# The last MoE column cut to two experts, its rows kept by quarters on partition groups and added to the tokens by 32-row products

## What is computed

```
x = rmsnorm(h_res)                                  # (512, 1024)
each token: the best of 4 groups, in it the best 2 of 8 experts, weights comb
for every expert e:  act = silu(x @ wg[e]) * (x @ wu[e]) * comb[:, e]
                     y  += act @ wd[e]              # wg, wu 1024x256, wd 256x1024
out = rmsnorm(h_res + y) * final_norm
```

## Time and profile before

| what | value |
|---|---|
| median of 3 runs | 498.78 us (497.97 to 499.63) |
| the profiled execution's own time | 497.26 us |
| its span | 495.4 us |
| mean granted clock of PE in the span | 0.989 of full speed |
| PE busy | 468.2 us (95%) |
| DVE busy | 282.6 us (57%) |
| ACT busy | 149.6 us (30%) |
| DMA bytes | 143.00 MB, mean 289 GB/s |

### The profile page before, as it was taken

The page is one execution under the profiler, slowest core; times in us unless marked ns, Lnnn a source line. Parts: engine busy times, 40 slices in busy tenths (PEclk is TensorE's granted clock), DMA queues, the critical chain, the costliest instruction groups (busy, mean ns, idle before and its releaser), DMA issues.

```text
span 495.4 us, 10550 instructions
## 1 busy us (share of the span) xinstructions
PE 468.2 (95%) x4290; PEld 312.1 (63%) x4290; DVE 282.6 (57%) x698; ACT 149.6 (30%) x367; POOL 37.3 (8%) x45
## 2 busy tenths in 40 slices
PE   7999999999999999998999999999999999885785
PEld 5888899888796544554656555655665555453442
DVE  4799999999967985248374422333342222132256
ACT  3450237630166333330244222221222121112134
POOL 0000000000001000000012021101202111000000
PEclk9999999999999999999999999999999999889999
DMA  8991000000008999539887999999999999999994
GB/s 270 351 370 61 1 0 2 1 1 1 3 3 278 413 427 426 251 103 415 324 305 266 420 384 429 422 420 424 419 425 420 424 419 425 422 425 425 419 372 182
DMA packets 29089, 143.00 MB, mean 289 GB/s; under 512 B 4357, under 2 KB 11685, under 8 KB 20336
## 3 DMA queue, kind: packets, MB, share of 16 engines
q1 hardware_dynamic: 23360, 131.03, 65.6%
q0 software_dynamic: 5248, 10.85, 6.2%
q10 hardware_dynamic: 432, 0.44, 0.3%
HBM read 133.21 MB, written 16.78 MB: 303 GB/s over the span
## 4 chain that ended last, share of the span: by engine, by line
PE 71%; DMA 17%; DVE 5%; SPq 4%; issue 1%; ACT 1%; DVEq 0%; ACTq 0%; POOLq 0%
PE bank_pair L1577 13%; PE bank_pair L1916 11%; PE bank_pair L1778 9%; DMA area_g<-in_w_exp 8%; DMA area_w<-in_w_exp 7%; PE bank_pair L1939 5%; PE bank_pair L1587 4%; PE bank_pair L1924 4%; PE bank_pair L1527 3%; SPq L519 3%; PE bank_pair L1715 3%; DVE area_m L934 2%; PE bank_pair L1909 2%; PE bank_pair L1947 2%; PE bank_pair L1542 1%; PE bank_pair L2369 1%
## 5 line engine op out<-in xcount | busy, mean ns | idle before, releaser
L1778 PE MATMUL bank_pair<-area_w,area_m 128*128 128x512 f32 x128 | 57.0, 595 | 0.0
L934 DVE SCALAR_TENSOR_TENSOR area_m<-area_g,cols,area_m 128x512 f32<-128x512 f32 x60 | 41.3, 744 | 0.0
L1778 PEld LDWEIGHTS bank_pair<-area_w,area_m 128*128 128x128 f32 x128 | 23.5, 190 | 26.0 <-issue 26.0
L1916 PE MATMUL bank_pair<-area_w,area_m 128*64 128x256 f32 x320 | 38.5, 383 | 1.4 <-DMA area_w<-in_w_exp 1.0
L1916 PE MATMUL bank_pair<-area_g,area_m 128*64 128x256 f32 x256 | 32.0, 393 | 2.1 <-DMA area_g<-in_w_exp 1.9
L1916 PEld LDWEIGHTS bank_pair<-area_w,area_m 128*64 128x64 f32 x320 | 22.4, 137 | 16.0 <-issue 5.9
L2152 DVE COPY cst<-bank_pair 128x128 f32<-128x128 f32 (+1 forms) x36 | 9.5, 263 | 36.0 <-PE bank_pair L1930 29.5
L2170 DVE COPY area_m<-bank_pair 64x512 f32<-64x512 f32 x20 | 13.9, 694 | 22.8 <-PE bank_pair L1939 22.8
L1916 PEld LDWEIGHTS bank_pair<-area_g,area_m 128*64 128x64 f32 x256 | 18.0, 139 | 13.9 <-issue 5.6
L2159 DVE TENSOR_TENSOR cst<-cst,bank_pair 128x128 f32<-128x128 f32 x22 | 6.4, 289 | 32.6 <-ACT cst L2073 32.6
L2161 DVE TENSOR_TENSOR cst<-cst,bank_pair 64x128 f32<-64x128 f32 x18 | 5.3, 293 | 32.0 <-ACT cst L2075 31.9
(11 more groups left out here) (443 smaller groups left out, 875.3 us busy)
## 6 DMA issues: line engine op xcount, KB each, us to landing
area_g<-in_w_exp SPq DMA_DIRECT2D x14, 2048.0 KB
area_w<-in_w_exp SPq DMA_DIRECT2D x13, 2048.0 KB, 37.8
area_w<-in_w_exp SPq DMA_DIRECT2D x16, 1024.0 KB, 8.3
area_g<-in_w_exp SPq DMA_DIRECT2D x14, 1024.0 KB
area_x<-in_w_exp SPq DMA_DIRECT2D x4, 2048.0 KB, 25.4
area_w<-in_w_in SPq DMA_DIRECT2D x6, 1024.0 KB, 14.1
area_w<-in_w_out SPq DMA_DIRECT2D x2, 2048.0 KB, 14.9
expert_out<-area_g SPq DMA_DIRECT2D x2, 2048.0 KB, 22.8
```

The costliest lines, as they stand in the source:

```text
L934: ins = V.scalar_tensor_tensor(out=mixT[:, i, :], in0=src, scalar=w, in1=mixT[:, i, :], op0=ALU.mult, op1=ALU.add)
L1778: ins = T.matmul(bank[7][:, :], mixT[:, k, j * P:(j + 1) * P], w_out_sb[:, n, k, :], start=(k == 0), stop=(k == KT - 1))
L1916: ins = T.matmul(out_b[h * BC:(h + 1) * BC, 0:2 * P], x[:, k, :], w_gate_up[slot][:, :, k, h * P:(h + 1) * P], start=(k == 0), stop=(k == ...
```

## The change

Columns 14 and 15 change places: the one with four light experts comes first (blocks 34 to 37) and is scattered, and the last has two (blocks 38 and 39; `OWN` is 38). A result of the last column keeps the form that `down_small` gives it: quarter q of the 1024 outputs on partitions 32q to 32q+31. So ACT copies it in one instruction (`y_quarters`), and `mix` is turned once for each of the two experts onto all four partition groups (`last_rows_turned(n)`, 16 small matmuls in blocks 35 and 37, and a copy by DVE each). The rows are added by 32-row products of 256 columns on the four row groups (`last_rows(n, j, q)`): 16 for each expert. Ten of the first expert's go between blocks 38 and 39 (`rows_before_last`), four behind block 39's gate and up, and two with the second expert's 16 behind its down product (`rows_of_last`). PSUM is laid out anew in two tensors of four banks; block 39 does all its work in bank 7. The residuals of tiles 0 and 2 go in before block 38's gate and up (three quarters) and behind its down product. The reads get semaphores by expert, tile 3's residual is read ahead of tile 2's rows, tile 2's first read is added by PE, the additions are whole tiles on DVE, and the tiles end in the order 1, 0, 2, 3. `keep_warm` goes. The core of the diff:

```diff
-    plan += [mid[1], light[0], heavy[0], heavy[1], light[1], heavy[2], mid[2], heavy[3], mid[3], mid[4], light[3], light[2]]
+    plan += [mid[1], light[0], heavy[0], heavy[1], light[1], heavy[2], mid[2], heavy[3], mid[3], mid[4], light[2], light[3]]
...
+        bank_quad = [ctx.enter_context(nc.psum_tensor(f"bank_quad{i}", [P, 2048], F32)) for i in range(2)]
+        bank = [bank_quad[i // 4][:, i % 4 * 512:(i % 4 + 1) * 512] for i in range(8)]
...
+        of_quarter = [gathered[:, n * SEQ:(n + 1) * SEQ] for n in range(2)]
...
-            def last_rows_turned():
-                dve.wait_ge(mix_turned, 1)
-                V.tensor_copy(mix_flat, bank[7][:, :]).then_inc(mix_ready, 1)
+            def last_rows_turned(n):
+                dve.wait_ge(mix_turned, 3 + n)
+                V.tensor_copy(of_quarter[n], bank[7][:, :]).then_inc(mix_ready, 1)
...
-        MIX_BANK = ((2, 3), (1, 6), (7, 0), (4, 5))
         AHEAD_TILE = 1
         BACK = (AHEAD_TILE, 0, 2, 3)
-        total = bank_pair[2][:, :]
-        weight_of = area_x[:, 0:2 * P].rearrange("p (k n) -> p k n", k=2)
+        FINAL = (AHEAD_TILE, 0, 2, 3)
+        QUARTER = D // 4
+        total = [bank_quad[0][:, :].rearrange("p (n c) -> p n c", n=4)[:, :, j * QUARTER:(j + 1) * QUARTER] for j in range(2)]
+        total += [bank_quad[1][:, j * D:(j + 1) * D].rearrange("p (n c) -> p n c", n=4) for j in range(2)]
+        yq = [area_m[:, 2 * KT * P + LAST % 2 * D + n * QUARTER:2 * KT * P + LAST % 2 * D + (n + 1) * QUARTER] for n in range(2)]
+        weight_of = area_x[:, 0:3 * P].rearrange("p (k n) -> p k n", k=3)
+        d_back = [[d_win[j] for j in range(NT)], d_x]
         ROOM_FROM = max(LAST_OF[RING - 1::RING]) + 1
-        SUMS = 2 * ET
...
+        def gu_bank(b_):
+            return bank[b_ % 2][:, 0:2 * P] if b_ < NB - 1 else bank[7][:, 0:P]
+        def turn_bank(b_):
+            return bank[4] if b_ < NB - 1 else bank[7][:, P:]
+        def down_bank(b_):
+            return bank[5 + b_ % 2] if b_ < NB - 1 else bank[7][:, QUARTER:]
...
-                if with_resid and j == ET:
-                    queue.dma_start(xr[j], resid[j * P:(j + 1) * P, :]).then_inc(d_spill, 16)
+                if with_resid and j == 2:
+                    queue.dma_start(xr[ET], resid[ET * P:, :]).then_inc(d_spill, 16)
                 for k in range(2):
-                    queue.dma_start(ye[k][:, j, :], expert_out[k * SEQ + j * P:k * SEQ + (j + 1) * P, :]).then_inc(d_x[j], 16)
+                    queue.dma_start(ye[k][:, j, :], expert_out[k * SEQ + j * P:k * SEQ + (j + 1) * P, :]).then_inc(d_back[k][j], 16)
...
-            for j in range(NT):
-                sp.wait_ge(o_ready, j + 1)
+            for i, j in enumerate(FINAL):
+                sp.wait_ge(o_ready, i + 1)
...
-            for b_ in range(OWN, NB):
-                y_out(b_ - 1)
-                silu_of(b_)
+            def y_quarters(b_):
+                act.wait_ge(dn_done, b_ + 1)
+                if b_ == OWN:
+                    act.wait_ge(d_sc[LAST % 2], sent(LAST - 2))
+                A_.activation(yq[b_ - OWN], down_bank(b_)[:, 0:QUARTER], ACT.Copy).then_inc(y_lo, 1)
+            y_out(OWN - 1)
+            silu_of(OWN)
+            y_quarters(OWN)
+            silu_of(NB - 1)
             act_turned(NB - 1)
-            y_both(NB - 1)
+            y_quarters(NB - 1)
...
-            for j in range(ET):
-                act.wait_ge(summed, j + 1)
-                row_stats(j, 0, xr[j])
-            act.wait_ge(mixed, 2 * ET + 1)
-            row_stats(ET, 0, total)
+            for i, j in enumerate(FINAL[:ET]):
+                act.wait_ge(summed, i + 1)
+                row_stats(i, j, by_quarter(xr[j]))
+            act.wait_ge(mixed, ALL_ROWS + 2)
+            row_stats(ET, ET, total[ET])
...
+                V.tensor_scalar(weight_of[:, 2, :], ident, w_rest[:, 0, 2:3], None, ALU.mult).then_inc(diag_ready, 1)
...
-                if b_ == MIX_AT + NT + 1:
-                    last_rows_turned()
+                if b_ == OWN - 2:
+                    last_rows_turned(0)
...
-            for b_ in range(OWN, NB):
-                act_turned(b_ - 1)
-                y_out(b_ - 1)
-                gated(b_)
-                if b_ == NB - 2:
-                    row_weights()
+            act_turned(OWN - 1)
+            y_out(OWN - 1)
+            gated(OWN)
+            row_weights()
+            last_rows_turned(1)
+            act_turned(OWN)
+            gated(NB - 1)
...
             def rows_ahead(j):
-                dve.wait_ge(d_x[j], 16 + 32)
                 for k in range(2):
+                    dve.wait_ge(d_back[k][j], 32)
                     V.scalar_tensor_tensor(out=xr[j], in0=ye[k][:, j, :], scalar=w_rest[:, k, j:j + 1], in1=xr[j],
                                            op0=ALU.mult, op1=ALU.add).then_inc(first_sum, 1)
                     dve.wait_ge(first_sum, k + 1)
             def last_added(j):
-                dve.wait_ge(mixed, 2 * j + 2)
...
+                dve.wait_ge(mixed, ALL_ROWS)
+                V.tensor_tensor(by_quarter(xr[j]), total[j], by_quarter(xr[j]), ALU.add).then_inc(summed, 1)
             def token_sums(j):
-                dve.wait_ge(d_x[j], 16 + 32)
...
+                dve.wait_ge(d_back[0][j], 32)
+                dve.wait_ge(mixed, ALL_ROWS)
+                V.scalar_tensor_tensor(out=by_quarter(xr[j]), in0=by_quarter(ye[0][:, j, :]), scalar=w_rest[:, 0, j:j + 1],
+                                       in1=total[j], op0=ALU.mult, op1=ALU.add).then_inc(first_sum, 1)
+                dve.wait_ge(d_back[1][j], 32)
+                dve.wait_ge(first_sum, SUMS)
                 V.scalar_tensor_tensor(out=xr[j], in0=ye[1][:, j, :], scalar=w_rest[:, 1, j:j + 1], in1=xr[j],
                                        op0=ALU.mult, op1=ALU.add).then_inc(summed, 1)
+            def second_added(j):
+                dve.wait_ge(d_back[1][j], 32)
+                dve.wait_ge(mixed, ALL_ROWS + 1)
+                V.scalar_tensor_tensor(out=by_quarter(xr[j]), in0=by_quarter(ye[1][:, j, :]), scalar=w_rest[:, 1, j:j + 1],
+                                       in1=total[j], op0=ALU.mult, op1=ALU.add).then_inc(summed, 1)
...
             rows_ahead(AHEAD_TILE)
+            last_added(AHEAD_TILE)
             token_sums(0)
-            last_added(AHEAD_TILE)
-            token_sums(2)
-            for j in range(ET):
-                row_norm(j, 0, xr[j])
-            row_norm(ET, 0, total)
+            row_norm(0, AHEAD_TILE, by_quarter(xr[AHEAD_TILE]))
+            second_added(2)
+            row_norm(1, 0, by_quarter(xr[0]))
+            row_norm(2, 2, by_quarter(xr[2]))
+            row_norm(ET, ET, total[ET])
...
-            def last_rows_turned():
+            def last_rows_turned(n):
                 pe.wait_ge(mix_made, NT)
+                pe.wait_ge(mix_ready, 2 + n)
                 for j in range(NT):
-                    ins = T.transpose(bank[7][:, j * P:(j + 1) * P], mix[:, j, :], ident)
+                    for q in range(4):
+                        ins = T.matmul(bank[7][q * 32:(q + 1) * 32, j * P:(j + 1) * P], mix[:, j, n * 32:(n + 1) * 32], ident,
+                                       start=True, stop=True, tile_position=(0, q * 32))
                 ins.then_inc(mix_turned, 1)
...
-            def keep_warm(n, width):
...
+            def resid_in(j, h, start):
+                T.matmul(bank_of(j, h), ident, xr[j][:, h * 512:(h + 1) * 512], start=start, stop=False)
+            def resid_quarter(q):
+                T.matmul(total[0][:, q, :], ident, by_quarter(xr[0])[:, q, :], start=True, stop=False)
+            def last_rows(n, j, q, start=False, stop=False):
+                p = slice(q * 32, (q + 1) * 32)
+                return T.matmul(total[j][:, q, :], of_quarter[n][p, j * P:(j + 1) * P], yq[n][p, :],
+                                start=start, stop=stop, tile_position=(q * 32, 0))
...
+            def rows_of_choice(k, j, weight, stop):
+                for h in range(2):
+                    ins = T.matmul(bank_of(j, h), weight, ye[k][:, j, h * 512:(h + 1) * 512], start=False, stop=stop)
+                return ins
+            def rows_before_last():
+                last_rows(0, 2, 0)
+                last_rows(0, 3, 1, start=True)
+                last_rows(0, 2, 2).then_inc(mixed, 1)
+                for q in range(4):
+                    last_rows(0, 0, q)
+                pe.wait_ge(mixed, 1)
+                last_rows(0, 3, 0)
+                last_rows(0, 2, 1)
+                last_rows(0, 2, 3).then_inc(mixed, 1)
+            def rows_of_last():
+                pe.wait_ge(mixed, 2)
+                last_rows(1, 2, 0)
+                last_rows(1, 3, 1)
+                last_rows(1, 2, 2)
+                last_rows(0, 3, 3, start=True).then_inc(mixed, 1)
+                last_rows(1, 0, 0)
+                last_rows(1, 0, 1)
+                last_rows(1, 0, 2)
```

(88 more changed lines are left out.)

82 lines of the change are left out of this document (30 added, 52 removed).

## The result

The changed kernel takes 502.61 us (median of 10 runs, 501.62 to 506.57), the kernel before in the same session 498.51 us (10 runs, 495.09 to 501.38). The ratio is 1.0094, with a 95% interval of 1.0067 to 1.0121; ratios are worked out from the fast runs of both kernels and can stand a little off the quotient of the two medians, here 1.0082. The forecast was 500.4 and slower: right in direction and inside its range, but 4.1 us were added where 1.6 us had been worked out. Measured again in two later sessions the same kernel came out at 1.0038 and 1.0044, with medians 1.5 and 1.95 us apart.

What follows compares the result with a forecast made beforehand. Expert weights bound the second half, so gains lay in the 24.1 us tail. ACT on tile 3 1.05 us later plus 0.6 for stores made 1.6 us: 498.9 profiled, 500.4 as median, range 497.4 to 503.0.

Steps and rivals of the forecast that it cites:

- The way of the reads: End of the kernel: reads behind the last scatter let PE finish at 490.6, 0.8 us later than before.
- The way of the engines: DVE and ACT behind the last rows: ACT takes up tile 3 at 490.9, 1.05 us later than before.
- Copies and last rows: Behind block 39's down product: one ACT copy gains 1.2 us, 18 products in 2.1 us gain 5.0 us.
- rival 4: Last column's 32-row products run one after another, not side by side: 9 us more, 509; chance 0.06.
- From block 39 to ACT on tile 3: Last stretch of the kernel: block 39 starts at 475.5 and ACT takes up tile 3 at 490.9.
- The reads: Reads wait for the last scatter: first issued at 474.4, landed at 478.2, the others every 1.26 us after.
- Rival 2: Last scatter needs its full 9.55 us, to 476.6: all reads 2.2 us later, PE idle, 502.6; chance 0.12.
- Rival 1: Scatter lands by about 472.5, reads land 2 us earlier, block 37 keeps full clock: not slower, 498.2; chance 0.27.
- Stores: At the end, tile 3's two halves may queue behind tile 2's store: between 0 and 1.2 us, taken 0.6.
- Block 39's start: Block 39 starts at 475.5, not 471.47, behind longer work in blocks 37 and 38: 4.0 us lost.
- rival 3: Clock falls in the tail, at block 38's waits or the reads' wait: up to 1.7 us, 502.1; chance 0.12.
- theory B: From the experiments, not the prediction: the change also delays the weights' last landing, by about 1 to 2 us.

Runs made afterwards that it cites:

- e10: Changed kernel, all outputs, with five filler products on PE ahead of block 37 and DVE copying block 38's turned result first; 501.28 us, 1.0082.
- e5: Changed kernel without column 14's scatter, four light experts missing from the output, reads issued earlier; 502.11 us, 1.0060.
- e7: Changed kernel without column 14's scatter and with DVE copying block 38's turned result before making the weight matrices; 499.19 us, 1.0000.
- e8: Changed kernel without column 14's scatter, DVE copying block 38's turned result first, five filler products on PE ahead of block 37; 498.39 us, 1.0006.
- e1: Changed kernel measured again, unaltered, against the kernel before; 499.63 us, 1.0038.
- e6: Changed kernel with DVE copying block 38's turned result before the weight matrices and the second turned matrix; 501.77 us, 1.0066.
- e9: Changed kernel measured a third time, unaltered, against the kernel before; 499.89 us, 1.0044.
- e12: Changed kernel without column 14's scatter, with DVE adding tile 2's second read ahead of tile 1's norm; 499.43 us, 1.0039.
- e11: Kernel before with the last block's product copied from PSUM in two halves, by ACT and DVE, instead of ACT's four copies; 496.96 us, 0.9993.
- e3: Kernel before with columns 14 and 15 exchanged and nothing else; 500.96 us, 1.0065.

## Why the prediction was right and where it was wrong

**Two ways to the last norm.** The traces of the changed kernel and its variants with all outputs fit one rule to 0.2 us, e10 apart: the last norm starts 16.93 us behind block 39 (by DVE and ACT) or 19.07 us behind the issue of the first read, whichever is later. It is a fit with two sizes taken from the same four traces; only the 16.93 stands in others too (e5, e7 and e8).

| trace | block 39 behind first read | block 39 to last norm | first read to last norm |
|---|---|---|---|
| changed | 2.98 | 16.93 | 19.91 |
| e1 | 2.46 | 17.11 | 19.57 |
| e6 | 1.72 | 17.36 | 19.08 |
| e9 | 1.20 | 17.86 | 19.06 |
| e10 (clock falls behind the wait) | -0.30 | 20.51 | 20.21 |

Before, the last norm started 491.55 - 471.33 = 20.22 us behind the landing. The way of the reads now gives 2.17 + 19.07 = 21.24, that is +1.02 us; the prediction had +0.8. The way of the engines gives 5.15 + 16.93 = 22.08, +1.86, in its first trace; the prediction had +1.05 and called the ways nearly even. They are, within 1 us: the way of the engines is the longer by 0.84 us in the first trace and 0.32 in e1, and the shorter by 0.94 in e9. With the engines' way shortened the reads hold the end (e6, and e10 with the fall of the clock beside), and e12 shows that it is DVE and ACT which bind the engines' way.

**Point by point.**
- *Copies and last rows:* right. From block 39's start to ACT's one copy done 4.8 us, as forecast, then 2.44 us of PE for the 18 products (forecast 2.1); rival 4, one after another, is out. The Trainium skill, "TensorE: Matmul & The Clock Gate", Packing small matmuls, has 3.07 times for four together, by which the estimate was 2.5; by that figure, the trace agrees.
- *From block 39 to ACT on tile 3:* forecast 475.5 to 490.9, 15.4 us; measured 479.10 to 494.34, 15.24. Right.
- *The reads:* the first was forecast 3.07 us behind the landing of the last gate and up weights and came 2.17 behind it; from there to the norm of tile 3 the forecast had 17.9 (474.4, PE's end 490.6, 1.7 of ACT), measured 19.07. The two errors of about 1 us cancel. Rival 2's 9.55 us for the scatter didn't come in the first two traces (7.71 and 7.93) and nearly came in e9 (9.05, the first read at 476.54), where the reads then bound. Rival 1 didn't come; its 498.2 also leaves out the 0.6 us of the stores.
- *Stores:* forecast +0.6; from the last norm to the end 3.88 us before, 4.66, 4.50 and 4.57 now. Right, slightly low.
- *Block 39's start:* the failed step, taken as 4.2 us behind the landing of the last gate and up weights and measured as 5.15 in the first trace. Block 37 to 38 was forecast at 9.86 us and took 9.58. Block 38 to 39 was forecast at 9.0 and took 11.04, 10.74 and 10.59. Without the fall of the clock it is 9.08 (e5). So the sum of the parts was right, though its 0.1 us for the switch to 32-row products stood on no row, and the second fall of the clock was left out: "my PE has no gap of over 1.5 us" was true (the gaps are 1.29, 0.69 and shorter), and no safeguard, since with these gaps PE was busy for 1.42 of 3.4 us and the clock fell behind it. What came was rival 3, with a chance of 0.12, and it cost 1.5 to 2.0 us, near its 1.7. It came in four of the five traces with DVE's old order and in none of the four where PE's wait of 1.29 us was shortened. The fifth, e5, had the same gaps and 1.39 of 3.4 us busy, and kept the clock; what decides between them isn't shown. Block 37 starting 0.8 us earlier against the last weights, which the prediction had not asked about, took some of it back. In the repeats the delay was 4.65 and, with block 37 at the full clock, 2.93 us, so over three traces its mean is 4.24, the 4.2 of the forecast: there the fall that was left out and the one that was put in and didn't come (e9) cancel by luck.
- *Ahead of the tail:* the forecast put everything up to the last landing at nothing. In the first trace that was 2.62 us, half of the 5.26 by which it ends later; why stays open, see below.

**The sum.** In the tail: forecast 1.05 + 0.6 = 1.65, measured 1.86 + 0.78 = 2.64 in the first trace, 2.0 as the mean of three. The mechanism and the sign were right, and in the first trace the term of block 39's start was undersized by 1 us. That is 1 us of the 2.5 by which the 4.1 us exceed the forecast; the other 1.5 lie ahead of the tail.

**What stays open.** The medians of the first session stand 4.1 us apart, and the tail explains 2.65. Most of the remainder was at the first issue of the expert loop (+1.50 us in that trace, +3.23 in e9's, but +0.37 in e1's), after code that is the same in both; the variants had 218.33 to 220.01 there. That points to spread between executions, and the two repeats near 1.004 fit it, but no run isolated it. From that issue to the last landing the traces of before and e11 take 250.5 to 251.8 us, and the nine of the changed kernel and its variants 251.7 to 253.0. The two groups hardly overlap: in each session with a trace of the kernel before or e11, the changed kernel's is the longer (by 1.12, 1.21 and 0.27 us), and the means are 1.0 us apart. So a slower stream of weights of about 1 us, theory B in small, is likely; with the tail's 2.0 it would make up the ratios' mean of 2.9. The swap alone doesn't show it (e3, 251.7), and no run isolated its cause. Single traces also can't stand for medians: e5's was its fastest run.

## What to carry to other kernels

Work moved off the end pays only until the next tied way: here 3.15 us came out of the last block's way, but the same edit made block 39 start 2.9 to 5.2 us behind its weights and pushed the last scatter from 450 to 468 us, and the reads behind it alone would have put the last norm 1.0 us later than before. Before taking a size from the chain, put a time on every way into the last instruction, measured from the event that nobody can move (the last weights), and on each separately. And where PE's work is cut into small pieces with hops between them, look at the busy time of a whole stretch and not only at its longest gap, and give a fall of the clock a real chance: here 1.42 us of 3.4, with no gap over 1.3 us, stood ahead of a fall that cost 1.5 to 2.0 us in four traces and didn't come in a fifth with the same gaps.

## What the runs showed that was not expected

- With five filler products in a wait for weights the clock stood at 1.00 and block 37 took 8.14 us instead of 10.72 (e8, e7), though e9 had 8.14 without them. Block 37 then starts behind the filler and not on its weights, 13.57 us ahead of the last landing instead of 14.97 (e8, e7), so that 1.2 us of it arrive at block 39.
- One wait for the fifth read costs twice: 2.70 us of waiting, and then the four records of the residual in 3.64 us instead of 1.98, because the clock fell behind the wait (e10).
- Twenty records of 32-row products of 256 columns took 1.56 us and 36 took 2.44, the same to 0.01 us in all nine traces of the changed kernel and its variants. At 0.215 us a record one after another the 36 would need 7.7.
